# The last head pair's cached keys and values stored from SBUF, and masks spread on chip

## What is computed

```python
proj = einsum('btd,de->bte', x, w_in)       # q, k, v, g_att, b, c, h, g_conv: 512 wide each
k_all = concatenate([k_past, k], axis=1); v_all = concatenate([v_past, v], axis=1)
# branches (window, dilation) = (128, 1), (512, 4), (2048, 16), merged by softmax denominators
att = dilated_attention(q, k_all, v_all, offset) * silu(g_att)
u_pad = concatenate([conv_past, c * h]);  z = b * conv3(u_pad) * silu(g_conv)
out = concatenate([att, z], -1) @ w_out
y = layer_norm(ALPHA * x + out, ln_g, ln_b)
new_k, new_v, new_conv = k_all[:, -2048:], v_all[:, -2048:], u_pad[:, t:]
```

## Time and profile before

| | us |
|---|---|
| median of 3 executions | 354.07 |
| lowest, highest | 353.64, 355.96 |
| the profiled execution | 354.37 |
| its span, first to last instruction | 352.6 |
| TensorE busy | 343.4 |
| VectorE busy | 201.1 |
| ScalarE busy | 117.1 |
| GpSimd busy | 10.9 |

### The profile page before, as it was taken

How to read it: one execution, slowest core, us unless ns; L and a number is a source line. 1 busy time by engine, 2 the same in 40 slices (tenths; PEclk the granted TensorE clock), 3 DMA queues, 4 the chain that set the end, 5 groups by cost and what they waited for, 6 DMA issues and landing times.

```text
span 352.6 us, 7188 instructions
## 1 busy us (share of the span) xinstructions
PE 343.4 (97%) x3024; PEld 297.6 (84%) x3024; DVE 201.1 (57%) x381; ACT 117.1 (33%) x233; POOL 10.9 (3%) x28
## 2 busy tenths in 40 slices
PE   8999999999999999999999999999999999999991
PEld 6998887998889889988898899888888877888791
DVE  3734518955144658651346486613546699794774
ACT  5623324342144333421442425213433644310100
POOL 0000000000100000001000000010000000200000
PEclk9999999999999999999999999999999999999997
DMA  7999999999999999999999999999999999999996
GB/s 295 401 425 416 415 422 418 423 423 418 424 411 423 423 418 410 362 417 418 414 414 422 422 409 341 418 415 404 425 416 418 418 405 342 364 399 385 396 355 256
DMA packets 31570, 141.03 MB, mean 400 GB/s; under 512 B 3121, under 2 KB 3505, under 8 KB 26545
## 3 DMA queue, kind: packets, MB, share of 16 engines
q1 hardware_dynamic: 15890, 76.34, 53.1%
q10 hardware_dynamic: 15648, 64.23, 46.7%
HBM read 132.66 MB, written 71.86 MB: 580 GB/s over the span
## 4 chain that ended last, share of the span: by engine, by line
PE 81%; DMA 9%; DVE 5%; ACT 2%; issue 1%; ACTq 0%; DVEq 0%
PE pj_b L1178 9%; DMA w_raw<-in_w_tiles 9%; PE pj_b L1180 8%; PE pj_b L1179 8%; PE pj_a L1178 7%; PE pj_a L1179 6%; PE pj_a L1180 6%; PE sc L1367 4%; PE sc L1333 4%; PE px L1524 3%; PE px L1526 3%; PE px L1525 3%; PE po L1313 2%; PE px L1282 2%; PE pt L1299 2%; DVE rg L917 1%
## 5 line engine op out<-in xcount | busy, mean ns | idle before, releaser
L1178 PE MATMUL pj_b<-x_hi,w_hi 128*128 128x320 f32 x248 | 78.5, 317 | 0.3 <-DVE mix L933 0.3
L1180 PE MATMUL pj_b<-x_hi,w_lo 128*128 128x320 f32 x248 | 76.5, 309 | 0.0
L1179 PE MATMUL pj_b<-x_lo,w_hi 128*128 128x320 f32 x248 | 76.5, 308 | 0.0
L1178 PE MATMUL pj_a<-x_hi,w_hi 128*128 128x256 f32 (+1 forms) x248 | 71.5, 288 | 0.0
L1180 PE MATMUL pj_a<-x_hi,w_lo 128*128 128x256 f32 (+1 forms) x248 | 69.4, 280 | 0.0
L1179 PE MATMUL pj_a<-x_lo,w_hi 128*128 128x256 f32 (+1 forms) x248 | 69.3, 280 | 0.0
L810 DVE TENSOR_TENSOR w_lo<-w_raw,w_hi 128x1024 fp32r<-128x1024 f32 x30 | 36.7, 1223 | 27.8 <-ACT w_hi L497 27.8
L1178 PEld LDWEIGHTS pj_a<-x_hi,w_hi 128*128 128x128 f32 x248 | 46.9, 189 | 6.1 <-issue 5.6
L1178 PEld LDWEIGHTS pj_b<-x_hi,w_hi 128*128 128x128 f32 x248 | 46.5, 188 | 5.7 <-issue 4.5
L497 ACT CAST w_hi<-w_raw 128x1024 fp32r<-128x1024 f32 x30 | 31.3, 1045 | 57.8 <-PE pj_b L1180 40.2
L1180 PEld LDWEIGHTS pj_a<-x_hi,w_lo 128*128 128x128 f32 x248 | 46.6, 188 | 0.0
(11 more groups left out here) (169 smaller groups left out, 457.5 us busy)
## 6 DMA issues: line engine op xcount, KB each, us to landing
k_buf<-in_k_used SPq DMA_DIRECT2D x16, 1280.0 KB, 13.4
v_buf<-in_v_used SPq DMA_DIRECT2D x20, 1024.0 KB, 14.1
out_k_used_out<-in_k_used ACTq DMA_DIRECT2D x16, 1280.0 KB, 20.9
out_v_used_out<-in_v_used ACTq DMA_DIRECT2D x17, 1024.0 KB, 15.6
w_raw<-in_w_tiles SPq DMA_DIRECT2D x30, 512.0 KB, 9.9
out_k_rest_out<-in_k_rest ACTq DMA_DIRECT2D x12, 1024.0 KB, 13.9
out_v_rest_out<-in_v_rest ACTq DMA_DIRECT2D x12, 1024.0 KB, 14.8
wo_raw<-in_w_out SPq DMA_DIRECT2D x8, 512.0 KB, 13.1
```

The costliest lines, as they stand in the source:

```text
L1178: nc.tensor.matmul(out, w_hi[:, w], x_hi[:, c], start=(k == 0), stop=False)
L1179: nc.tensor.matmul(out, w_hi[:, w], x_lo[:, c], start=False, stop=False)
L1180: return nc.tensor.matmul(out, w_lo[:, w], x_hi[:, c], start=False, stop=(k == KT - 1))
```

## The change

Three things are changed.

*Keys.* The last pair's four key pieces are no longer copied from HBM to HBM. ScalarE issues a store of each from `k_buf`, `store_k(c)`, after a wait that the piece has been loaded: pieces 0 and 1 in round 2 and piece 2 in the last, in the places of copies, and piece 3 behind the second step's exponentials. SyncE waits for the store of each (`k_stored`) before it loads w_out over it.

*Values.* The last pair's value pieces 0 and 1 are stored from `v_buf` like 2, 3 and 4. SyncE issues 0, 1 and 2 together and waits for all three before it loads ln_g and ln_b, and so before all that stands behind.

There are 51 copies in place of 57; the list is the same but for these six, so the later ones move up.

*Masks.* The left half of `mask_pr` repeats a pattern of 16 columns, and in the first 1,024 columns of `mask_s` 96 of each 128 are equal. The parts come in one load of 280 columns into `p_s`, and GpSimd makes the two regions out of them with three copies; the rest of either mask is loaded as before. VectorE waits for them (`masks_made`).

```diff
+OLD = 3 * P // 4
+FAR = SEQ - 2 * P
+PATTERN = 16
+M_NEAR = 8 * (P - OLD)
+M_COLS = 8 + PATTERN + M_NEAR
...
-STORED = (2, 3, 4)
-N_COPIES = 2 * REST_ROWS + NPAIR * (K_PIECES + V_LOADS) - len(STORED)
+N_COPIES = 2 * REST_ROWS + (NPAIR - 1) * (K_PIECES + V_LOADS)
...
+SMALL = 6 * 16
...
+        def repeated(a, columns):
+
+            return bass.AP(tensor=a.tensor, offset=a.offset, ap=[[S_COLS, P]] + columns)
...
-            for tensor, name in ((ident, "ident"), (mask_pr, "mask_pr"), (state, "state"), (conv_w, "conv_w")):
+            for tensor, name in ((ident, "ident"), (state, "state"), (conv_w, "conv_w")):
                 sp.dma_start(tensor[:, :], d[name]).then_inc(small_in, 16)
-            sp.dma_start(mask_s[:, :], d["mask_s"]).then_inc(small_in, 16)
+            sp.dma_start(mask_pr[:, FAR:], d["mask_pr"]).then_inc(small_in, 16)
+            sp.dma_start(p_s[:, 0:M_COLS], d["mask_parts"]).then_inc(small_in, 16)
+            sp.dma_start(mask_s[:, 8 * P:], d["mask_s"]).then_inc(small_in, 16)
...
             sp.wait_ge(k_used, pieces + 1)
+            sp.wait_ge(k_stored[0], 16)
             load_wo(0)
             load_v(NPAIR - 1, 2)
             load_w(W_TILES - 1)
             sp.wait_ge(k_used, pieces + 2)
+            sp.wait_ge(k_stored[1], 16)
             load_wo(1)
             load_v(NPAIR - 1, 3)
             sp.wait_ge(k_used, pieces + 3)
+            sp.wait_ge(k_stored[2], 16)
             load_wo(2)
             load_v(NPAIR - 1, 4)
             sp.wait_ge(k_used, pieces + 4)
+            sp.wait_ge(k_stored[3], 16)
             load_wo(3)
...
-            store_values(2)
+            for m in range(3):
+                store_values(m)
 
 
             sp.wait_ge(s_pv, NPAIR)
             sp.wait_ge(vn_saved, 16 * NPAIR)
+            sp.wait_ge(v_stored, 16 * 3)
             sp.dma_start(y_t[0:1, 0:2 * D_MODEL], d["ln_gb"]).then_inc(ln_in, 16)
...
-            sp.wait_ge(v_stored, 16 * len(STORED))
+            sp.wait_ge(v_stored, 16 * V_LOADS)
...
-            pool.wait_ge(small_in, 80)
+            pool.wait_ge(small_in, SMALL)
+            pool.tensor_copy(mask_pr[:, 0:FAR].rearrange("p (n c) -> p n c", c=PATTERN),
+                             repeated(p_s[:, 8:8 + PATTERN], [[0, FAR // PATTERN], [1, PATTERN]])).then_inc(masks_made, 1)
+            old_new = mask_s[:, 0:8 * P].rearrange("p (r n) -> p r n", n=P)
+            pool.tensor_copy(old_new[:, :, 0:OLD], repeated(p_s[:, 0:8], [[1, 8], [0, OLD]])).then_inc(masks_made, 1)
+            pool.tensor_copy(old_new[:, :, OLD:], p_s[:, 8 + PATTERN:M_COLS].rearrange("p (r n) -> p r n", r=8))\
+                .then_inc(masks_made, 1)
...
+            def store_k(c):
+                n = K_PIECES * (NPAIR - 1) + c
+                act.wait_ge(k_in[c], 16 * NPAIR)
+                act.dma_start(d["k_used_out"][n * P:(n + 1) * P, :], k_buf[:, c * K_SLOT:(c + 1) * K_SLOT])\
+                    .then_inc(k_stored[c], 16)
...
                 copy_q(i + 1)
-                copy_next()
+                if i < NPAIR - 2:
+                    copy_next()
+                else:
+                    store_k(0)
                 split_hi(t0 + 8)
-                copy_next()
+                if i < NPAIR - 2:
+                    copy_next()
+                else:
+                    store_k(1)
...
                 copy_c(i, 0)
-                copy_next()
+                store_k(2)
                 out_sample_turned(i - 1)
                 exp_prompt(i, 0)
                 copy_c(i, 1)
                 move_prompt(i, 0)
                 exp_prompt(i, 1)
+                store_k(3)
                 split_hi(t0 + 2)
                 move_prompt(i, 1)
                 exp_prompt(i, 2)
                 split_hi(t0 + 3)
-                copy_next()
...
-                if t < 3:
+                if t < 1:
                     copy_next()
...
-            dve.wait_ge(small_in, 80)
+            dve.wait_ge(small_in, SMALL)
+            dve.wait_ge(masks_made, 3)
...
-                    pe.wait_ge(small_in, 80)
+                    pe.wait_ge(small_in, SMALL)
```

More of the change, by code:

```diff
@@ L167, in layer_step @@
             sem("k_saved"), sem("v_saved"), sem("vn_saved"), sem("copied"), sem("conv_out"))
-        v_stored = sem("v_stored")
+        v_stored, k_stored = sem("v_stored"), [sem(f"k_stored{c}") for c in range(K_PIECES)]
         y_out = [sem(f"y_out{n}") for n in range(Y_SLOTS)]
-        blank = sem("blank")
+        blank, masks_made = sem("blank"), sem("masks_made")
         x_hi_done, x_lo_done = sem("x_hi_done"), sem("x_lo_done")
@@ L544, in copy_next @@
                     copy_rest(n)
-                elif n < N_COPIES - NPAIR * K_PIECES:
+                elif n < N_COPIES - (NPAIR - 1) * K_PIECES:
                     n -= 2 * REST_ROWS
@@ L548, in copy_next @@
                 else:
-                    n -= N_COPIES - NPAIR * K_PIECES
+                    n -= N_COPIES - (NPAIR - 1) * K_PIECES
                     copy_k(n // K_PIECES, n % K_PIECES)
@@ L1554, in mask_arrays @@
     scaled = [np.maximum(m / SCALE, NEG).astype(np.float32) for m in (np.concatenate([mask_s, new], 1), mask_pr)]
-    return dict(zip(("mask_s", "mask_pr"), scaled))
+    used, near = scaled
+    old = used[:, 0:8 * P].reshape(P, 8, P)
+    assert (old[:, :, 0:OLD] == old[:, :, 0:1]).all()
+    assert (near[:, 0:FAR].reshape(P, -1, PATTERN) == near[:, None, 0:PATTERN]).all()
+    parts = np.concatenate([old[:, :, 0], near[:, 0:PATTERN], old[:, :, OLD:].reshape(P, M_NEAR)], 1)
+    return {"mask_parts": parts, "mask_s": used[:, 8 * P:], "mask_pr": near[:, FAR:]}
 def split_cache(c):
```

## The result

| | before | after |
|---|---|---|
| median of 4 executions, us | 354.72 | 364.50 |
| lowest, highest | 353.64, 355.96 | 362.87, 366.62 |
| ratio, 95% interval | | 1.0281 (1.0244 to 1.0317) |
| the profiled execution | 354.37 | 364.39 |
| its span | 352.6 | 362.6 |

A forecast was written before the change was run, and what follows sets the result against it. TensorE's order was taken to set the time, DMA only where a late transfer holds TensorE. Terms -0.76 + 0.9 - 0.1 = 0.0 gave 354.1 us, from the median of 354.07; range 352.9 to 357.5.

The forecast's parts named there:

- The masks: Round 0: fewer mask bytes loaded remove its 0.76 us excess; GpSimd's copies, 2.5 us, are hidden.
- the late weight tile: Round 0: a weight tile held up TensorE's sample scores; landing up to 1.3 us earlier, it gives back 0.76 us.
- The key stores: Round 2's end and the last round: stores and waits on ScalarE and SyncE are covered and cost nothing.
- recover by 275: SyncE's loads of w_out, last values and last weight tile: up to 3 us later in the middle, then caught up.
- A full load is a full load: Six HBM-to-HBM copies, 7.3 MB, become stores of the same bytes; the 16 engines stay as full, only the timing changes.
- The value stores: SyncE's wait before the LayerNorm vectors: 2.10 MB more at 0.23 MB/us, landing 9.0 us later, at 302.0.
- the residual comes much too late: First residual: stores at 0.162 MB/us, residual lands at 317.8, TensorE stands 4.9 us; +4.0, 358.1 us; chance 0.07.
- Equal bytes: Value stores: queues share by bytes, residual at 315.2, TensorE stands 2.3 us; +1.4, 355.5 us; chance 0.17.
- Residual, sum, TensorE: Third output tile: residual takes 11.0 us, landing at 313.8, the sum 2.0 more; TensorE stands 0.9 us.
- What follows absorbs the delay: After the third output tile's start: VectorE needs less time per tile than TensorE, so no further loss.
- ScalarE: Before the output tiles: 4 us longer at its full queue, VectorE at the first sum at 311.5, costing nothing more.
- The end: Last output store: fewer copies beside it leave emptier engines, a gain of 0.1 us (none to 0.4).

The follow-up runs named there:

- the keys alone: The changed kernel with the values as before, without the wait for value stores; key stores and masks kept: 353.87 us, ratio 1.0005.
- the values alone: The changed kernel with the keys as before; value stores, their wait and masks kept: 360.52 us, ratio 1.0207.
- the moved wait: The changed kernel with SyncE's wait for the three value stores put behind the first residual, ahead of the second: 353.50 us, ratio 0.9988.
- masks alone: The kernel before with the masks spread on chip and nothing else of the change: 353.77 us, ratio 1.0000.
- the filled gap: The changed kernel with 34 useless 512-column matmuls added in TensorE's gap ahead of the third output tile: 361.18 us, ratio 1.0188.
- the two runs on rows: The changed kernel with key copies' rows cut from 5 to 2.5 KB (367.16 us), or with value stores' rows cut from 8 to 4 KB (370.52 us).
- The stores behind the residual: The changed kernel with value stores 0 and 1 and the wait issued behind the first residual, store 2 left at 271: 357.70 us, ratio 1.0048.
- the two-store kernel: The changed kernel with value piece 0 copied as before, so two value stores instead of three stand ahead of the wait: 355.22 us, ratio 0.9964.
- the short copy rows: The changed kernel with the twelve key copies on ScalarE's queue in rows of 2.5 KB in place of 5 KB: 367.16 us, ratio 1.0360.
- without late copies: The changed kernel with the last 12 copies of ScalarE's queue left out, so less work is done: 353.53 us, ratio 0.9924.

## Why the prediction was wrong

The place and the mechanism were right: the price lies at the value stores, passes through the vectors' load and the first residual to VectorE's first sum, and meets TensorE at its third output tile. The size was wrong by a factor of nine there, and one term was missing.

**The masks** (-0.76): 0.54 by the start of the last round's scores, 243.34 against 243.88. In this execution the late weight tile was not the way: round 0 still takes 71.97 us (28.50 to 100.47) and ScalarE still stands 9.0 us for its tile; 0.32 us came before the first scores. The traces of the kernels with the same masks differ (round 0 of 71.42 us with the keys alone, 71.33 with the values alone, 72.47 with the moved wait), and masks alone have a ratio of 1.0000 (0.9971 to 1.0030), so a gain of this size is not shown. GpSimd's copies took 2.5 us (16.24 to 18.75), as reckoned.

**The key stores** (nothing): right for the kernel that has them alone. Wrong in a half-sentence, that SyncE's loads "recover by 275". They don't, since the queue has no idle time in which to recover: w_out's first piece is issued at 245.74 and lands at 267.8, 6.1 us later than before, its last 6.8. The fourth key piece was near its limit: it landed at 253.86, where 249.5 and 4 us more were allowed for, and its store was issued at 253.88. The split behind it ran at 254.32, 0.8 us later than before, and TensorE lost nothing by it.

**A full load is a full load** (no term): not in bytes. From 304 to 314 the copies had the engines of after nearly to themselves:

```profile
q10 hardware_dynamic: 679, 3.27, 98.2%
```

That is 0.33 MB/us; with both queues at work it was 0.42 (2.54 MB from 284 to 290). So what a busy engine carries depends on the kind of transfer. What this was worth in the tail was not looked into.

**The value stores** (9.0 us later; the step that failed, the landing of the stores as the old landing plus two stores' bytes). The last store landed 16.7 us later (309.7 against 293.0). The start of that sum was already wrong by 6.8, as above: 2.4 on 15 of the engines, the rest for one engine that lags. The split is that of one execution: in the traces of the moved wait and of the filled gap, the same kernel up to there, w_out's last piece is 5.1 and 4.2 us later than before, with a lag of 0.9 and 1.1. What remains, 9.9 us for 2.10 MB, is 0.21 MB/us, near the rate assumed. So it wasn't the share that was missed but the start of the stores, and that the landing counts by the slowest engine. The rival *the residual comes much too late* named that engine in passing and put no number to it: it came out at 317.8 for the residual, measured 321.5. *Equal bytes* falls with the two runs on rows.

**Residual, sum, TensorE** (11.0 and 2.0): 11.0 and 2.05. TensorE arrived 0.54 earlier, at 315.08, so that it stood 8.6 us in place of 0.9.

**What follows absorbs the delay**: it absorbed the first tile's, and with the wait moved all of it. The stores behind the residual show its limit, the slot of y_t, which the prediction had listed among what would prove it wrong.

**The clock** (no term): 2.48 us. At a stall of 0.9 us it costs nothing, as the two-store kernel shows at 1.6. The kernel with the values alone lost its clock after 5.1 us. In the rival with 4.9 us a term for it was due, and the range's upper end, 357.5, lacked it.

**ScalarE** (4 us longer in front of its queue, VectorE at the sum at 311.5): 9.85 us against 6.59, VectorE ready at 312.5, hidden behind the residual.

**The end** (-0.1): -0.60. The last y store lands 2.0 us after its issue in place of 2.6. That is also less than the 2.6 us of the formula that the prediction quotes from the Trainium skill, DMA: Bandwidth & Descriptors, Anatomy of one DMA, which is a fit for transfers issued from GpSimd; this store is SyncE's. With fewer copies beside it, the sums, the issues and the other half of y end sooner too; how the 0.6 divide was not looked into.

## What to carry to other kernels

Before a wait goes onto a DMA-issuing queue, list what is queued behind it and put those loads that don't need it in front; here the place of that one line was worth some 10 us. Where a transfer's landing is on the path, don't add bytes at a mean rate to an old landing: the transfers ahead of it in its queue shift too once the other queue's work moves, and the last of 16 engines counts, up to 6 us behind the others here. A stall of TensorE can cost a start at half its clock besides (2.5 us here). A remedy that gives one queue a larger share can hand the wait to the engine that issues on the other, as the short copy rows did.

## What the hardware showed that was not expected

- One of the 16 DMA engines ran behind on SyncE's queue while both queues had work: 1.3 us at w_out's last piece in before, 5.7 in after, 0 to 5.9 in the kernels tried, 0.1 with the masks alone and 0.1 without late copies. It is there with the values alone (4.5) and with the keys alone (3.6), and not the same in kernels that differ only after that point (5.7, 1.1, 0.9). What makes it stays open.
- A residual of 512 KB took 9.8 to 11.6 us to land beside the copies (17.7 with three stores queued ahead of it) and 3.8 without them.
- TensorE's granted clock was 0.50 from 323.6 to 328.5, after the gap of 8.4 us, 0.51 from 320.6 to 324.9, after that of 5.1 (values alone), and 1.00 after a gap of 1.6 us (two stores).
- While both queues had work, equal numbers of their rows were moved (236 and 234, 274 and 272, 299 and 298 packets in 6 us), whatever the lengths, 2.5 to 8 KB.
- An issue on ScalarE's queue takes 0.58 us while there is room, and took 10.1 and 9.7 us with the same bytes cut into twice the rows. It came free with five copies of 256 rows not yet landed, or with two to three of 512.
- GpSimd copied 256 columns in 0.40 us and, from a strided source, in 1.40.
